# Gate, up and router weights loaded with eight neighbouring rows per partition, in a one-core hybrid decoder step

## What is computed

```
def rmsnorm(x, g):
    xf = x.astype(jnp.float32)
    y = xf * lax.rsqrt(jnp.mean(xf * xf, axis=-1, keepdims=True) + EPS)
    return (y * g.astype(jnp.float32)).astype(x.dtype)
...
    lg = (t @ w_rg).astype(jnp.float32) + b_rg
...
    le_all = jnp.einsum('td,gde->tge', t, w_re)
...
    hid = jax.nn.silu(jnp.einsum('td,edf->tef', t, w_gate)) * jnp.einsum('td,edf->tef', t, w_up)
    hid = hid * gates[..., None].astype(hid.dtype)
    out = jnp.einsum('tef,efd->td', hid, w_down)
...
    x = x + hier_moe(rmsnorm(x, norm2), w_rg, b_rg, w_re, b_re, w_gate, w_up, w_down)
```

## Time and profile before

| | |
|---|---|
| Time, median of 3 runs | 955.8 us (953.46 to 958.86) |
| Time of the profiled execution | 963.07 us |
| Its span | 960.9 us |
| TensorE busy | 808.8 us (84%) |
| VectorE busy | 566.1 us (59%) |
| ScalarE busy | 428.2 us (45%) |
| GpSimd busy | 262.0 us (27%) |
| Read from memory, written | 129.25 MB, 28.86 MB |
| DMA packets | 99073, of these 91170 on the queue of SP |

### The profile page before, as it was taken

The page is one execution under the profiler, slowest core; times in us unless marked ns, Lnnn a source line. Parts: engine busy times, 40 slices in busy tenths (PEclk is TensorE's granted clock), DMA queues, the critical chain, the costliest instruction groups (busy, mean ns, idle before and its releaser), DMA issues.

```text
span 960.9 us, 16136 instructions
## 1 busy us (share of the span) xinstructions
PE 808.8 (84%) x6200; PEld 508.4 (53%) x6200; DVE 566.1 (59%) x918; ACT 428.2 (45%) x772; POOL 262.0 (27%) x173
## 2 busy tenths in 40 slices
PE   4999989779979999867899999991589999887830
PEld 2766634336546644324566745541577786655710
DVE  6632587747654612088688644337657676766815
ACT  5431230245652312145576524423457566575714
POOL 2114995640502000020000100000514736424312
PEclk9999999979989999988899999995589999998975
DMA  8316875401022378843000123326776799999648
GB/s 297 93 49 196 238 245 170 159 0 36 10 91 74 113 228 264 267 156 110 1 1 1 34 99 132 133 89 229 235 257 196 250 280 279 313 297 291 167 82 326
DMA packets 99073, 155.86 MB, mean 162 GB/s; under 512 B 13704, under 2 KB 63384, under 8 KB 98994
## 3 DMA queue, kind: packets, MB, share of 16 engines
q1 hardware_dynamic: 91170, 132.92, 42.0%
q0 software_dynamic: 6208, 18.17, 7.7%
q10 hardware_dynamic: 1616, 3.70, 1.0%
HBM read 129.25 MB, written 28.86 MB: 165 GB/s over the span
## 4 chain that ended last, share of the span: by engine, by line
PE 51%; DVE 14%; DMA 12%; issue 9%; POOL 6%; ACT 5%; SPq 2%; POOLq 0%; DVEq 0%; ACTq 0%
PE ps L2140 13%; PE ps L2142 12%; PE ps L2141 12%; DMA hT_reg<-h_scratch,tok 5%; POOL kv L866 4%; DMA sum_scratch<-kv,dest 3%; PE ps L2462 2%; DVE mxs L1745 2%; PE ps L2342 1%; DMA gt<-q_scratch 1%; DVE w_reg L1442 1%; DVE dg_reg L2132 1%; PE ps L2450 1%; PE ps L2547 1%; PE ps L2283 1%
## 5 line engine op out<-in xcount | busy, mean ns | idle before, releaser
L936 POOL DMA_INDIRECT sum_scratch<-kv,dest x26 | 72.5, 2790 | 124.5 <-DMA sum_scratch<-kv,dest 79.2
L2140 PE MATMUL ps<-hT_reg,w_reg 128*128 128x344 f16 (+1 forms) x312 | 98.4, 315 | 2.6 <-DVE hT_reg L1454 2.6
L2141 PE MATMUL ps<-hT_reg,w_reg 128*128 128x344 f16 (+1 forms) x312 | 98.3, 315 | 0.0
L2142 PE MATMUL ps<-hT_reg,w_reg 128*128 128x344 f16 (+1 forms) x312 | 98.1, 314 | 0.0
L866 POOL TENSOR_TENSOR kv<-kv,gt 128x1024 f32<-128x1024 f32 x32 | 83.1, 2620 | 52.9 <-DMA kv<-in_cache_k 52.7
L2140 PE MATMUL ps<-w_reg,hT_reg 128*128 128x512 f16 x192 | 74.7, 389 | 10.5 <-ACT kv L1111 6.8
L894 POOL TENSOR_TENSOR rst<-rst,neghalf 128x1 f32<-128x1 f32 (+3 forms) x27 | 18.9, 699 | 230.0 <-DVE rst L1726 230.0
L2141 PE MATMUL ps<-w_reg,hT_reg 128*128 128x512 f16 x192 | 74.4, 388 | 0.0
L2142 PE MATMUL ps<-w_reg,hT_reg 128*128 128x512 f16 x192 | 74.2, 387 | 0.0
L1215 ACT ACTIVATE hT_reg<-ps,mxn 128x128 f32<-128x128 f32 (+7 forms) x64 | 47.1, 738 | 52.9 <-DVE mxn L1746 52.1
L2140 PE MATMUL ps<-hT_reg,dg_reg 128*128 128x128 f16 (+4 forms) x256 | 55.2, 239 | 1.9 <-DVE hT_reg L2004 1.9
(11 more groups left out here) (403 smaller groups left out, 2116.3 us busy)
## 6 DMA issues: line engine op xcount, KB each, us to landing
kv<-in_cache_k SPq DMA_DIRECT2D x64, 256.0 KB, 3.5
w_reg<-in_w_gate SPq DMA_DIRECT2D x16, 1024.0 KB
w_reg<-in_w_up SPq DMA_DIRECT2D x16, 1024.0 KB
w_reg<-in_w_down SPq DMA_DIRECT2D x16, 1024.0 KB, 14.3
w_reg<-in_w_in SPq DMA_DIRECT2D x12, 1024.0 KB, 6.7
mix_reg<-in_cache_v SPq DMA_DIRECT2D x32, 256.0 KB, 3.1
kv<-in_cache_v SPq DMA_DIRECT2D x32, 256.0 KB, 3.1
mix_reg<-in_x_prompt SPq DMA_DIRECT2D x8, 512.0 KB, 8.6
```

The source lines that it names most:

```text
L936: pool.indirect_dma_start(out=sumd[:, :], out_offset=bass.IndirectOffsetOnAxis(ap=dest[0:r, 2 * e + g:2 * e + g + 1], axis=0), in_=yb[0:r, ...
L2140: pe.matmul(out, lh, rh, start=start, stop=False)
L2141: pe.matmul(out, lh, rl, start=False, stop=False)
L2142: return pe.matmul(out, ll, rh, start=False, stop=stop)
```

## The change

The weights of gate, up and router are loaded so that partition p holds rows 8 p to 8 p + 7. For gate and up that is one piece of 8 KB in memory per partition. So that column and row still meet, the norm writes column 8 q + k of a row to place 128 k + q of h2: the reads of `x1` and the gain stay in order, and successive writes go to places 128 elements (512 B) apart. The rest, w_down too, is as before. The columns in `h_scratch` are then in the new order.

```
--- before
+++ after
...
-                sp.dma_start(wr[:, :, 0:NG], I["w_router_g"][0].rearrange("(k p) g -> p k g", p=P)).then_inc(s_par, 16)
+                sp.dma_start(wr[:, :, 0:NG], I["w_router_g"][0].rearrange("(p k) g -> p k g", p=P)).then_inc(s_par, 16)
                 for g in range(NG):
                     sp.dma_start(wr[:, :, NG + EPG * g:NG + EPG * (g + 1)],
-                                 I["w_router_e"][0, g].rearrange("(k p) e -> p k e", p=P)).then_inc(s_par, 16)
+                                 I["w_router_e"][0, g].rearrange("(p k) e -> p k e", p=P)).then_inc(s_par, 16)
...
             def load(w, sub, x, s, sems):
-                src = I[w][0, x].rearrange("e (k p) f -> p (e k) f", p=P)
+                src = I[w][0, x].rearrange("e (k p) f -> p (e k) f" if w == "w_down" else "e (p k) f -> p (e k) f", p=P)
...
-                        src = w[0, bass.ds(e, 1)].rearrange("e (k p) f -> p (e k) f", p=P)
+                        src = w[0, bass.ds(e, 1)].rearrange("e (k p) f -> p (e k) f" if i == 2 else
+                                                            "e (p k) f -> p (e k) f", p=P)
...
-                dve.scalar_tensor_tensor(h2[0:r, t % 2], x1[0:r, t], rst[0:r, t:t + 1], gbc[0:r], ALU.mult,
-                                         ALU.mult).then_inc(s_h2, 1)
+                by_chunk = h2[0:r, t % 2].rearrange("p (k q) -> p q k", k=KC)
+                x1q, gq2 = [v.rearrange("p (q k) -> p q k", k=KC) for v in (x1[0:r, t], gbc[0:r])]
+                dve.scalar_tensor_tensor(by_chunk, x1q, rst[0:r, t:t + 1], gq2, ALU.mult, ALU.mult).then_inc(s_h2, 1)
```

## The result

The changed kernel takes 964.22 us (median of 14 runs, 958.18 to 971.09) beside 957.5 us for the kernel before (14 runs, 953.46 to 963.15). The ratio is 1.007, with a 95% interval of 1.0049 to 1.0091: **slower by 0.7%**, where 951.6 us, a gain of 0.4% and a range of 943 to 964 had been forecast. The profiled execution took 967.08 us, a span of 964.9.

What follows compares the result with a forecast made beforehand. From 820 to 900 us it saw the kernel waiting on scatter and gather, slowed by weight bursts sharing the DMA engines. 963.07 - 5.4 (waits) - 0.4 (first gather) + 1.6 (norm) = 958.9, in median terms 951.6 us; range 943 to 964.

Steps and rivals of the forecast that it cites:

- The packet count: Hardware queue: 28,700 fewer packets, from 32 gate and up loads going from 1024 rows to 128.
- The rate: Gate and up loads: 8 KB rows move at 414 GB/s instead of 348, 0.96 us less per expert.
- The slow start: Start of each weight burst: fewer, longer rows remove 0.25 us, bounds 0 and 0.7.
- All five waits on tokens stand behind such a burst. Four ... give it back whole: TensorE, 740 to 900 us: four waits each shorten by 1.2 us, the fifth by 0.6.
- The term of -5.4 us: Expert loop, 740 to 900 us: total saving in TensorE's waits on gathered tokens, 5.4 us.
- The first gather: Start of the experts: its data starts 0.4 us earlier because first weights leave the queue sooner; bounds 0 and 1.9.
- Today landings come at the end of all of it: Late expert rounds: landings already follow all an engine's work in a round, an argument against small transfers being held up.
- The holding-up rival: Late rounds: long weight rows delay scatters, 1.3 us in each of six rounds, 965.0 us in median terms; chance 0.14.
- The norm: End of the norm stage: strided writes cost 0.8 us more per norm, two on the path, 1.6 us.
- The base: Whole kernel: the profiled 963.07 us is 7.3 above the median, carried over unchanged to the forecast.
- The waits on tokens: TensorE, 740 to 900 us: 13.6 us falls to about 8; near 0 if gains compound, above 15 if held up.
- The router's loads: Router's five DMAs: same pieces expected, with nearly 20 us of slack, so an effect of 0.

Runs made afterwards that it cites:

- loads8: Kernel before with only gate's and up's loads changed to 8 KB rows, norm and router loads as before; ratio 1.0072 to the kernel before.
- after: The changed kernel itself, first trace, against the kernel before: median 964.22 us, profiled execution 967.08 us.
- after2: The changed kernel, unchanged, timed and traced once more: 962.32 us, ratio 1.0062 to the kernel before.
- before: The kernel before the change; the first trace, on which the prediction rested, took 963.07 us; median beside the changed kernel 957.5 us.
- norm_only: Changed norm and router loads, with gate and up loaded in 1 KB rows as in the kernel before; ratio 1.0006 to it.
- after_down1: The changed kernel with w_down's pieces cut from 4 KB to 1 KB; ratios 0.9982 and, repeated, 0.9991 to the kernel before.
- early8: Kernel before with gate and up in 8 KB rows for experts 0 to 8 only; ratio 0.9987 to the kernel before.
- loads2: Kernel before with gate and up in 2 KB rows instead of 1 KB; ratio 1.0052 to the kernel before.
- late8: Kernel before with gate and up in 8 KB rows for experts 9 to 15 only; ratio 1.0020 to the kernel before.
- before2: The kernel before, unchanged, timed and traced a second time; ratio 0.9991 to itself.

## Why the prediction was wrong, point by point

**The packet count** held to the last hundred: 28,672 fewer, 28,700 forecast.

**The rate** held where weights run alone: 414 GB/s had been taken for 8 KB, and 429 was measured. In the late bursts, where it was to pay, it was 388 against 343, an estimated 0.7 us a burst (2.10 MB) and not 0.96. The Trainium skill's count of overhead cycles ("DMA: Bandwidth & Descriptors", "Why small descriptors are slow"), which gave a gap of 7.5%, was too small for either pair (23% and 13%). **The slow start** of a burst, 0.25 us of the 1.2, shows no clear gain: shares of 0.70, 0.86 and 0.65 in first full microseconds after (825, 842 and 872 us), 0.79, 0.59 and 0.67 before.

**"All five waits on tokens stand behind such a burst. Four ... give it back whole"** is the step that failed. It took the burst for one block that scatter and gather come out of 1.2 us sooner. In fact they take turns with it, and their pace depends on the piece next to them: 0.28 MB in 2 us beside w_down's 4 KB, 0.37 beside 1 KB. The term of -5.4 us had the wrong sign: loads8, the loads alone, costs 0.72%, about 7 us, the waits on tokens did not fall (14.4 and 13.1 us, 13.6 and 12.6 before), and with w_down in 1 KB pieces the loss is gone. That the pieces' lengths make the loss is shown by these runs; by which waits it reaches the end is known only in part.

**The first gather**, to start 0.4 us earlier, starts 2.5 and 3.3 us later in after and after2 (678.99 and 679.81 us, 676.54 in before), and its data takes as long (6.12 and 6.29 us, 6.18 in the earlier trace rows): the term shows nowhere.

**"Today landings come at the end of all of it"**, the reason against the holding-up rival, was wrong too. In before the scatter issued at 854.51 has landed by 863.96, when the next one is issued, and from 863 to 866 us another 366 weight packets pass beside 22 software ones.

**The holding-up rival** (965.0, 964.2 measured) had the right sign and place, and the right size by luck: it had a wrong mechanism for most of its price. It let the scatter's first packets wait for the whole burst, 7.6 us; they still come at some 5 us, whatever the pieces are. Its other half, the one-for-one turns, was thought to cost nothing, since 8 KB pieces would be gone by then; the 4 KB pieces of w_down, which the change doesn't touch, were not priced. It had a chance of 0.14. The Trainium skill ("DMA: Bandwidth & Descriptors", section "Queues, rings and completion order") lets an engine drain 9 to 17 descriptors of one ring before it switches. The traces disagree: 69 to 64, 99 to 97 and 124 to 124, and 41 to 41 within one microsecond of 16 engines.

**The norm**: 0.8 us more forecast, 0.71 measured, so the write side pays as the Trainium skill says ("SBUF — State Buffer", "Door 1: The DMA port swizzle"). Two norms on the path, 1.6 us, may be short: the first gather comes at 678.6 to 679.9 in the five traces of norm_only, after, after2 and the two of after_down1, and at 676.5 in both traces of before. But without the strided norm it ranges from 674.2 (early8) to 680.7 (loads2) and 684.6 (late8), so one trace says little. In the time it can't be resolved (norm_only +0.06%, interval 0.47% wide).

**The base** was a second, hidden error. The profiled execution's 7.3 us above the median were carried over as a constant. In before2, whose time is the median's, the loop is 5.4 us shorter: the surplus sat in the rounds whose waits the prediction meant to shorten, though less in the waits (13.6 against 12.6 us) than in the clock (5.1 against 1.7 withheld).

**The waits on tokens**, forecast 8, above 15 if held up, were 14.4: the indicator did not tell the cases apart, since waits of the same total were followed by more of the lower clock. The prediction had priced that clock (3 us behind the 5.35 us wait) only as something to win back. **The router's loads** showed nothing, as forecast.

## What to carry to other kernels

Where a small transfer on the critical path shares the DMA engines with bulk loads, look at the packet size that it takes turns with, not only at the bulk's rate: shorter pieces beside it can be worth more than bandwidth that nobody waits for, down to the length at which the bulk itself comes late (here 1 KB still helped, 512 B did not). Making bulk transfers faster also changes what runs beside the small one. And take a second trace before pricing waits of a few microseconds, and hold what a trace shows against the executions that were only timed: the stretch that makes one execution slower than the median may be the very one you mean to improve.

## What was not expected of the hardware

- TensorE fell to 1.2 GHz behind waits of 1.92 us (before2, 897.69) and 2.22 us (after2, 841.51), and stayed at full clock behind one of 3.92 us (before2, 876.04).
- A transpose whose stationary operand is read at every eighth fp16 column takes 149 ns to load, against 103 in order.
- The first software packets follow a burst at about 5 us whether its pieces have 1 or 8 KB.
- With w_down in 512 B pieces the landing waits fall to 58.5 us, the DMA engines are full (1.01), ScalarE waits for weights, and the kernel is 0.35% slower.
